# A two-block transformer layer in float32: the norms by token tile, with a token-major slab behind each

## The chip, the cores and the metric

The kernel runs on one NeuronCore of a Trainium2 chip. The metric is the device time of one execution in microseconds. TensorE multiplies matrices, VectorE, ScalarE and GpSimd (POOL) compute beside it, and SyncE (SP) issues the transfers. PSUM has eight banks of 512 float32 columns on 128 partitions.

## The reference

Two transformer blocks run one behind the other over 256 tokens of width 1024, all in float32. The first block has MoBA attention and gated linear attention, and an FFN whose hidden values go through a causal convolution of three taps. A `final_norm_g` norm ends it. The second block begins with a norm of its own, so between the blocks stand two norms in a row. Its mixer has four branches (short convolution, spatial gating, stick-breaking attention, forgetting attention), and its FFN is a SwiGLU.

```python
def rms_norm(x, g):
    xf = x.astype(jnp.float32)
    y = xf * lax.rsqrt(jnp.mean(xf * xf, axis=-1, keepdims=True) + EPS)
    return (y * g.astype(jnp.float32)).astype(x.dtype)

# first block
        x = x + jnp.concatenate([y_moba, y_gla], axis=-1) @ w_out[l]
        hn = rms_norm(x, ffn_norm_g[l])
        h = causal_dwconv(hn @ w_ffn_up[l], conv_w[l], conv_b[l])
        h_gate, h_val = h[..., :D_FF], h[..., D_FF:]
        x = x + (jax.nn.silu(h_gate) * h_val) @ w_ffn_down[l]
    return rms_norm(x, final_norm_g)
# second block
        xn = _rms_norm(h, norm_mix_g[l])
        h = h + _mixer_block(xn, ...)
        h = h + _swiglu(_rms_norm(h, norm_ffn_g[l]), w_ffn_in[l], w_ffn_out[l])
```

## The kernel before

**Slabs.** All large weights arrive as 117 slabs of 1 MB (`STREAM`, 128 x 2048). An "up" slab holds 256 output columns for all 1024 inputs, a "down" slab 256 inputs for all 1024 outputs. Each is split into a high half that the fast float32 product takes exactly (ScalarE, `rnd`, to `hiw`) and the remainder (VectorE, `res`, to `low`). Both are rings of three. A product of two float32 matrices is thus three: high x high, high x low, low x high (`three`). A slab's high half waits until the slab three before it has been used (`consumed`).

**Order.** No planner is at work: each engine's program is written out by hand, in one order per engine, with semaphores between them. What stands later in an engine's program waits for what stands earlier.

**Stages.** In order: in1, out1, norm 1, FFN 1, norm 2, in2 (11 projections sq, sk, sv, fq, ... and 8 early gates), mix2, norm 3, FFN 2, output. FFN slabs are g and v (up, gate and value) and d (down), f = 0 to 10; the order is `FFN_ORDER`. In the FFN an up slab is made feature-major: weights stand, and 512 columns, high and low tokens side by side (`xx`), move (`feature_major_wide`, into two banks, 16 products of 512 columns and 16 of 256). VectorE reduces the two banks. A down slab (`out_slab`) adds to four accumulators, the quarters q = 0 to 3: token tile q // 2 (128 tokens), output half q % 2. A quarter takes 6 products of 512 columns. The last three down slabs, d8, d9, d10, come in a row behind the last up slab. `g_lo_ffn1` says that VectorE has made the low half (`ylo`) of a hidden slab.

**A norm.** `out_slab` gives `first_tile_out` after quarter 1 of its last slab. VectorE adds quarters 0 and 1 to the residual `h`, and quarters 2 and 3 once the whole slab is done. ScalarE squares and sums tile 0 and half of tile 1 (`norm_stats`), VectorE the other half (`norm_tile1`), POOL takes the inverse root (`inverse_roots`), VectorE scales the rows (`norm_scaled`), and TensorE transposes 16 blocks of 128x128 into four banks (`turn`). Ahead of these it multiplies zeros (`keep_clock`; 11, 19 and 13 calls at norms 1, 2 and 3, each two instructions in the trace). Then ScalarE makes the high half with the gain (`norm_turned`, 8 instructions of 128x256) and VectorE the low half. The first slab behind the norm starts as soon as the first pair of blocks is there. Norm 2 is the two norms in one: `weighted` multiplies `h` with `final_norm_g`, both sums of squares are taken, the rows scaled are the weighted ones, and `h` itself is rewritten behind (line 1205). At norm 1 the low split of slab v0 stands ahead of the norm in VectorE's program, at norm 3 between its additions.

Lines that the rows name: 593 ScalarE's high half of the norm; 984 VectorE's low half; 967 the additions to `h`; 939 VectorE's sum of squares; 948 the scaled rows; 1406 the transposes; 1393 the zeros; 932 and 563 the splits of a slab; 1146 the reduce of an up slab; 1182 the low half of y; 1417 to 1419 the three products; 1442 and 1448 the wide ones and their low part; 544 POOL's copies for the forgetting attention, which follow its roots of norm 2; 485 the output.

Of the kernel before, what the change touches and what calls it, by code (L numbers as in the profile page):

```python
# [17 lines left out]
ALU = mybir.AluOpType  # L18
# [5 lines left out]
P = 128  # L24
T = 256
# [31 lines left out]
WARM = [12, 11, 19, 13]  # L57
# [39 lines left out]
def build(nc, x_in, slabs_in, vec_in, cst_in, out):  # L97
    with ExitStack() as ctx:
# [57 lines left out]

        def norm_scale(n, tt):

            return stat(n, 10 + 2 * tt + (n == 2))

# [65 lines left out]

        def take_bank(pe, name):

            b, _, n, _ = lease[name]
            if n:  # L230
                pe.wait_ge(bank_free[b], n)
# [24 lines left out]
        for q in range(4):  # L256
            tenant(f"n1_{q}", (2, 5, 6, 7)[q], 2)
# [13 lines left out]
        for q in range(4):  # L271
            tenant(f"n2_{q}", 4 + q, 2)
        for n, b in (("sq", 0), ("sk", 1), ("sv", 0), ("fq", 6), ("fk", 7), ("fv", 1), ("cc", 0), ("cx", 1), ("cb", 0),
                     ("u", 1), ("v", 0)):
            tenant(n, b, 2 if n in ("fq", "fk") else 1)
# [23 lines left out]
        for q in range(4):  # L299
            tenant(f"n3_{q}", 4 + q, 2)  # L300
# [35 lines left out]
        def consumed(n, i=None):  # L336

            stage, name = STREAM[n]
            if stage in FREE:
# [22 lines left out]
        xs = piece(0, TT, D)  # L362
        hn = piece(12288, TT, D)
# [88 lines left out]
        def _(sp):  # L452
# [37 lines left out]
        def _(pool):  # L490
            me = Chain("pool_step")

            def inverse_roots(n, tt):

                pool.wait_ge(s(f"ssq{tt}_made"), (n + 1) * (1 + tt))
                mean = stat(n, 6 + 2 * tt)
                if tt == 0:
                    me.step(pool, pool.tensor_scalar(mean, stat(n, 0), EPS, None, ALU.add))  # L500
                else:
                    me.step(pool, pool.tensor_tensor(mean, stat(n, 1), stat(n, 2), ALU.add))
                wide = 1
                if n == 2:
                    wide = 2
                    me.step(pool, pool.tensor_scalar(stat(n, 7 + 2 * tt), mean, EPS, None, ALU.mult))
                    me.step(pool, pool.tensor_tensor(stat(n, 7 + 2 * tt), stat(n, 7 + 2 * tt), stat(n, 3 + tt), ALU.add))
                pool.tensor_tensor(stat(n, 10 + 2 * tt, wide), stat(n, 6 + 2 * tt, wide), mhalf[:, 0:wide],
                                   ALU.pow).then_inc(s("rstd_made"), 1)
# [12 lines left out]
            for tt in range(TT):  # L522
                inverse_roots(0, tt)
# [31 lines left out]
        def _(act):  # L555
# [13 lines left out]
            def norm_stats(n):  # L569

                act.wait_ge(*((s("h_made"), 4 * n - 2) if n else (s("x0_in"), 16)))
                def squares(dst, src, k):
                    return act.activation(dst, src, ACT.Square, scale=D ** -0.5, accum_out=stat(n, k))  # L573

                ins = squares(junk, h[:, 0, :], 0)
                if n == 2:
                    me.step(act, ins)
                    act.wait_ge(s("weighted"), 1)
                    ins = squares(junk, xs[:, 0, :], 3)
                ins.then_inc(s("ssq0_made"), 1)  # L580
                act.wait_ge(*((s("h_made"), 4 * n - 1) if n else (s("x1_in"), 16)))
                ins = squares(junk_act, h[:, 1, 0:D // 2], 1)
                if n == 2:
                    act.wait_ge(s("ssq0_made"), n + 1)
                    act.wait_ge(s("weighted"), 2)
                    ins = squares(junk, xs[:, 1, :], 4)
                ins.then_inc(s("ssq1_made"), 1)

            def norm_turned(n):

                for kt in range(KT):
                    act.wait_ge(*full(f"n{n}_{kt // 2}"))
# [11 lines left out]
            norm_stats(0)  # L604
# [5 lines left out]
            norm_turned(0)  # L610
# [129 lines left out]
            norm_stats(1)  # L740
            act.wait_ge(s("vec_rest_in"), 16)
            norm_turned(1)
# [53 lines left out]

            rnd(b2 + 1)
            norm_stats(2)
            norm_turned(2)
# [119 lines left out]
            norm_stats(3)  # L919
            norm_turned(3)  # L920
# [5 lines left out]
        def _(dve):  # L926
# [8 lines left out]
            def norm_tile1(n):  # L935

                dve.wait_ge(*((s("h_made"), 4 * n) if n else (s("x1_in"), 16)))
                half = h[:, 1, D // 2:]
                dve.tensor_tensor_reduce(junk_dve, half, half, 1.0 / D, EPS, ALU.mult, ALU.add,
                                         stat(n, 2)).then_inc(s("ssq1_made"), 1)  # L940

            def norm_scaled(n, tt):

                dve.wait_ge(s("rstd_made"), 2 * n + tt + 1)
                rows = xs if n == 2 else h
# [1008 lines left out]
```

## Time and profile before

| | |
|---|---|
| median of 3 runs | 752.34 us (752.27 to 753.6) |
| profiled execution | 752.77 us |
| its span | 751.0 us |
| TensorE busy (matmul) | 733.1 us, 98% |
| VectorE, ScalarE, POOL busy | 522.2, 374.6, 49.6 us |
| mean granted TensorE clock | 0.998 |
| read from HBM | 126.57 MB, 170 GB/s |

The span runs from the first to the last instruction; 1.8 us of the execution lie outside it. A product's duration in a row contains its pipeline: a 128x512 product is shown as 0.39 us, while the next one starts 0.23 behind it. Steps are therefore read from one start to the next.

### The profile page before, as it was taken

Reading aid. Unit: us, or ns where it says so; the run is one execution under the profiler, and the core shown is the slowest. Engines: PE = TensorE matmul, PEld = TensorE weight load, DVE = VectorE, ACT = ScalarE, POOL = GpSimd, SP = SyncE. Lnnn points to the kernel's source line nnn. Section 1 sums busy time; section 2 is a strip of 40 time slices with the busy share of each in tenths; the row PEclk is TensorE's granted clock in tenths of the full one; section 3 lists DMA queues with packets and bytes.
Section 4 is the critical chain, followed back from the end, with each engine's and each line's share of the span. In section 5 each row is a group of like instructions: output and inputs, shape, how many; then the busy total and the mean of one; then the engine's idle time right before and its main releaser. Section 6 shows DMA issues by size and latency. Waiting matters only on the chain.

```text
span 751.0 us, 11966 instructions
## 1 busy us (share of the span) xinstructions
PE 733.1 (98%) x4786; PEld 658.7 (88%) x4786; DVE 522.2 (70%) x587; ACT 374.6 (50%) x441; POOL 49.6 (7%) x64
## 2 busy tenths in 40 slices
PE   8999999899999999989999999999999999999997
PEld 7999887788888888879989999999978888888886
DVE  6679836689888888886557636675586766656673
ACT  6635466365554545555564554444445434444341
POOL 2456100100000000030000000000010000000000
PEclk9999999999999999999999999999999999999999
DMA  8836334236555555436343444446443655555431
GB/s 341 325 130 198 113 113 169 93 132 225 187 205 175 205 179 190 147 113 217 121 162 127 160 168 168 168 168 224 170 168 113 224 171 202 187 178 213 168 113 56
DMA packets 18810, 129.28 MB, mean 172 GB/s; under 512 B 2256, under 2 KB 2512, under 8 KB 3536
## 3 DMA queue, kind: packets, MB, share of 16 engines
q1 hardware_dynamic: 18768, 128.68, 48.1%
q8 instruction: 32, 0.52, 0.3%
q14 instruction: 10, 0.08, 0.0%
HBM read 126.57 MB, written 1.05 MB: 170 GB/s over the span
## 4 chain that ended last, share of the span: by engine, by line
PE 91%; DVE 5%; ACT 2%; POOL 1%; issue 1%; DMA 1%; POOLq 0%; DVEq 0%; ACTq 0%
PE ps L1442 21%; PE ps L1417 18%; PE ps L1418 18%; PE ps L1419 18%; PE ps L1448 11%; DVE xx L984 1%; DVE low L932 1%; PE ps L1540 1%; DVE h L967 1%; PE ps L1570 1%; DMA h<-in_x 1%; PE ps L1406 0%; ACT arena L573 0%; PE ps L1563 0%; ACT xx L593 0%
## 5 line engine op out<-in xcount | busy, mean ns | idle before, releaser
L932 DVE TENSOR_TENSOR low<-raw,hiw 128x2048 fp32r<-128x2048 f32 x116 | 268.3, 2314 | 117.7 <-ACT hiw L563 116.7
L563 ACT ACTIVATE hiw<-raw 128x2048 fp32r<-128x2048 f32 x116 | 221.9, 1914 | 176.8 <-PE ps L1448 114.9
L1442 PE MATMUL ps<-xx,hiw 128*128 128x512 f32 x704 | 170.8, 394 | 2.8 <-DVE xx L984 2.6
L1442 PEld LDWEIGHTS ps<-xx,hiw 128*128 128x128 f32 x704 | 131.0, 190 | 31.6 <-DVE xx L984 4.3
L1417 PE MATMUL ps<-xx,hiw 128*128 128x256 f32 x512 | 146.7, 286 | 0.5 <-DVE xx L984 0.5
L1418 PE MATMUL ps<-xx,hiw 128*128 128x256 f32 x512 | 144.8, 283 | 0.0
L1419 PE MATMUL ps<-xx,low 128*128 128x256 f32 x512 | 144.8, 283 | 0.0
L1417 PEld LDWEIGHTS ps<-xx,hiw 128*128 128x128 f32 x512 | 97.9, 191 | 2.4 <-issue 1.8
L1418 PEld LDWEIGHTS ps<-xx,hiw 128*128 128x128 f32 x512 | 97.9, 191 | 0.1
L1419 PEld LDWEIGHTS ps<-xx,low 128*128 128x128 f32 x512 | 97.9, 191 | 0.0
L1448 PEld LDWEIGHTS ps<-xx,low 128*128 128x128 f32 x704 | 90.3, 191 | 3.4
L1448 PE MATMUL ps<-xx,low 128*128 128x256 f32 x704 | 91.3, 283 | 0.0
L1417 PE MATMUL ps<-hiw,yhi 128*128 128x512 f32 x208 | 81.6, 392 | 0.5 <-DVE ylo L1096 0.5
L1418 PE MATMUL ps<-low,yhi 128*128 128x512 f32 x208 | 81.2, 390 | 0.0
L1419 PE MATMUL ps<-hiw,ylo 128*128 128x512 f32 x208 | 80.9, 389 | 0.0
L1146 DVE TENSOR_REDUCE arena<-ps 128x512 f32<-128x1024 f32 x44 | 53.8, 1222 | 32.4 <-PE ps L1448 32.3
L601 ACT ACTIVATE arena<-ps 128x512 f32<-128x512 f32 x37 | 22.1, 597 | 99.2 <-PE ps L1419 99.2
L1417 PEld LDWEIGHTS ps<-hiw,yhi 128*128 128x128 f32 x208 | 39.1, 188 | 8.9 <-DVE ylo L1096 0.8
L1419 PEld LDWEIGHTS ps<-hiw,ylo 128*128 128x128 f32 x208 | 39.1, 188 | 8.3
L1418 PEld LDWEIGHTS ps<-low,yhi 128*128 128x128 f32 x208 | 39.1, 188 | 7.3
L1168 DVE SCALAR_TENSOR_TENSOR arena<-arena,vec 128x255 f32<-128x255 f32 x88 | 40.5, 481 | 6.4 <-ACT arena L761 2.2
L1417 PE MATMUL ps<-hiw,xx 128*128 128x256 f32 x112 | 32.3, 288 | 0.0
(199 smaller groups left out, 802.7 us busy)
## 6 DMA issues: line engine op xcount, KB each, us to landing
raw<-in_slabs SPq DMA_DIRECT2D x117, 1024.0 KB, 4.8
vec<-in_vec SPq DMA_DIRECT2D x1, 1258.5 KB, 10.3
cst<-in_cst SPq DMA_DIRECT2D x1, 1220.0 KB, 13.7
h<-in_x SPq DMA_DIRECT2D x2, 512.0 KB, 4.2
arena<-arena SPq DMA_DIRECT2D x16, 64.0 KB, 3.1
out<-h SPq DMA_DIRECT2D x2, 512.0 KB, 2.6
vec<-in_vec SPq DMA_DIRECT2D x1, 229.0 KB, 4.6
cst<-in_cst SPq DMA_DIRECT2D x1, 66.0 KB, 4.3
```

Source lines behind the costliest of these rows:

```text
L563: act.activation(hiw[:, n % SPLIT, :], raw[:, n % RAW, :], ACT.Copy).then_inc(hi_made, 1)
L601: return act.activation(dst, src, func, scale=scale).then_inc(*frees(name))
L932: dve.tensor_tensor(low[:, n % SPLIT, :], raw[:, n % RAW, :], hiw[:, n % SPLIT, :].bitcast(F32), ALU.subtract).then_inc(lo_made, 1)
L967: dve.tensor_tensor(dst, ps[:, acc, :], dst, ALU.add).then_inc(s("h_made"), 1)
L984: dve.scalar_tensor_tensor(out=xlo[:, kt, :], in0=bank(f"n{n}_{kt // 2}")[:, kt % 2 * T:(kt % 2 + 1) * T], scalar=V(f"ng{n}")[:, kt:kt + 1 ...
L1146: dve.tensor_reduce(dst, wide_hidden(j).rearrange("p c (a b) -> p c b a", a=2), AX_X, ALU.add).then_inc(hidden_free(k, f, j)[0], 1)
L1168: ins = dve.scalar_tensor_tensor(out=dst[:, o:], in0=src[:, 0:T - o], scalar=w, in1=dst[:, o:], op0=ALU.mult, op1=ALU.add)
L1417: pe.matmul(o, whi, mhi, start=start, stop=False)
L1418: pe.matmul(o, whi, mlo, start=False, stop=False)
L1419: return pe.matmul(o, wlo, mhi, start=False, stop=stop)
L1442: pe.matmul(banks[:, c, :], hi[:, kt, cc_], xx[:, kt].rearrange("p a b -> p (a b)"), start=kt == 0, stop=False)
L1448: mm = pe.matmul(banks[:, c, 0:T], lo[:, kt, cc_], xhi[:, kt, :], start=False, stop=kt == KT - 1)
```

## The change

Norms 1 to 3 go by token tile. VectorE adds quarter by quarter (`quarter`, on `quarter_out` after quarters 0, 1 and 2), each tile has its own sums, root, rows, transposes and halves, and ScalarE scales half of each tile's rows. Tile 1's eight transposes go to two banks (`turned_at`). The slab behind the norm (`TILED`: g0 of either FFN, sq in in2) is computed token-major, a tile at a time, by 24 products of 256 columns each (`tile_slab`); tile 1's transposes stand between tile 0's high and low products. ScalarE copies the result to SBUF (`rows_out`), and four transposes turn it back (`turn_back`): in the FFNs between v0's high and low products, in in2 between the two tiles of sv. VectorE takes g0 by a copy of 512 columns instead of a reduce. sk's products wait for the high half alone at first (`feature_major_late`). The zeros at norms 1 to 3 are gone.

At norm 2 the squares of `h` are kept (`squared`) and VectorE weights them with the square of `final_norm_g` in its sums; the gain of both norms is one vector, which POOL spreads (`gains`, behind norm 1's roots, with `fg2`) and VectorE joins after its second FFN 1 step. `h` is rewritten by a product of two tensors. FFN 1's d9 and d10 run tile by tile, with tile 0's transposes ahead of d10's last quarter. The output's second tile leaves in two halves.

```diff
-WARM = [12, 11, 19, 13]
+WARM = 12
+TILED = {1: [("ffn1", "g0")], 2: [("in2", "sq")], 3: [("ffn2", "g0")]}
...
             def inverse_roots(n, tt):
+                a = 8 * tt
+                if n == 2:
+                    pool.wait_ge(s("squares_made"), sums_until(n, tt))
...
+                else:
+                    pool.wait_ge(s("squares_made"), sums_until(n, tt))
+                    pool.wait_ge(s("half_summed"), sums_until(n, tt))
+                    me.step(pool, pool.tensor_tensor(stat(n, a + 2), stat(n, a), stat(n, a + 1), ALU.add))
+                    pool.tensor_tensor(norm_scale(n, tt), stat(n, a + 2), mhalf[:, 0:1], ALU.pow)\
+                        .then_inc(s("root_made"), 1)
...
+                if n == 1:
+                    pool.wait_ge(s("vec_rest_in"), 16)
+                    pool.tensor_tensor(gains, V("fg").rearrange("p (k c) -> p k c", k=KT),
+                                       ident.unsqueeze(1).broadcast_to([P, KT, P]), ALU.mult).then_inc(s("gains_spread"), 1)
+                    pool.tensor_tensor(fg2, V("fg"), V("fg"), ALU.mult).then_inc(s("gains_squared"), 1)
...
# ScalarE, norm 1 (norm 3 alike) and norm 2
+            for tt in range(TT):
+                square(1, tt, 0)
+                rows(1, tt)
+                tile_turned(1, tt)
+            for tt in range(TT):
+                rows_out(1, 0, tt)
...
+            for nh in range(2):
+                square(2, 0, nh)
+            rows(2, 0)
+            square(2, 1, 0)
+            tile_turned(2, 0)
+            square(2, 1, 1)
             rnd(b2 + 1)
+            rows(2, 1)
+            tile_turned(2, 1)
...
# VectorE
+            def norm(n, used):
+                quarter(n, 0, used)
+                quarter(n, 1, used)
+                half_sum(n, 0)
+                quarter(n, 2, used)
+                rows(n, 0)
+                quarter(n, 3, used)
+                half_sum(n, 1)
+                tile_turned(n, 0, range(0, 4))
+                rows(n, 1)
+                tile_turned(n, 0, range(4, 8))
+                tile_turned(n, 1, range(8))
+            def weighted_norm(used):
+                quarter(2, 0, used)
+                quarter(2, 1, used)
                 for nh in range(2):
+                    weighted_sum(0, nh)
+                quarter(2, 2, used)
+                rows(2, 0)
+                tile_turned(2, 0, range(0, 4))
+                quarter(2, 3, used)
+                tile_turned(2, 0, range(4, 8))
+                for nh in range(2):
+                    weighted_sum(1, nh)
+                rows(2, 1)
+                tile_turned(2, 1, range(8))
...
+            norm(1, (proj_used["out1"], 4))
             res(first_ffn + 1)
-            norm(1, (proj_used["out1"], 4))
             res(first_ffn + 2)
...
# TensorE
+            def tile_slab(norm, i, tt, middle=None):
+                name, n = f"rows{norm}_{i}_{tt}", AT[TILED[norm][i]]
+                hi, lo = slab_views(n, KT)
+                t_ = slice(tt * P, (tt + 1) * P)
+                take_bank(pe, name)
+                o = bank(name)[:, 0:256]
+                pe.wait_ge(lo_made, n + 1)
+                for kt in range(KT):
+                    if kt % 2 == 0:
+                        pe.wait_ge(s("xhi_made"), KT + 16 * (norm - 1) + 8 * tt + kt + 2)
+                    pe.matmul(o, xhi[:, kt, t_], hi[:, kt, :], start=kt == 0, stop=False)
+                    pe.matmul(o, xhi[:, kt, t_], lo[:, kt, :], start=False, stop=False)
+                if middle is not None:
+                    middle()
+                for kt in range(KT):
...
+                    mm = pe.matmul(o, xlo[:, kt, t_], hi[:, kt, :], start=False, stop=kt == KT - 1)
+                mm.then_inc(*fills(name))
...
+            def ffn_up_first(k):
+                norm, n = {"ffn1": 1, "ffn2": 3}[k], AT[(k, "v0")]
+                turn_tile(norm, 0)
+                tile_slab(norm, 0, 0, lambda: turn_tile(norm, 1))
+                tile_slab(norm, 0, 1)
+                def back():
+                    pe.wait_ge(*hidden_free(k, 0, 0, done=False))
+                    turn_back(norm, 0, wide_hidden(0)[:, 0, :]).then_inc(hidden_full(k, 0, 0)[0], 1)
...
+                feature_major_wide(wide_hidden(1), n, (lo_made, n + 1), back).then_inc(hidden_full(k, 0, 1)[0], 1)
...
+            def ffn_down_last_two(k):
+                for tt in range(TT):
+                    for f in (FF - 2, FF - 1):
+                        n, par = AT[(k, f"d{f}")], f % 2
+                        pe.wait_ge(s(f"g_lo_{k}"), f + 1)
+                        pe.wait_ge(lo_made, n + 1)
+                        for q in (2 * tt, 2 * tt + 1):
+                            if q == 3 and f == FF - 1:
+                                turn_tile(2, 0)
+                            mm = out_quarter(n, q, (2 * par, 2 * par + 1), yhi, ylo, bank(f"{k}_acc{q}"), False,
+                                             f == FF - 1)
```

## Rows read from the trace of the kernel before

**Rows 1.** The page, part 1: busy time, share and instructions of each engine.
```profile
PE 733.1 (98%) x4786; PEld 658.7 (88%) x4786; DVE 522.2 (70%) x587; ACT 374.6 (50%) x441; POOL 49.6 (7%) x64
```

**Rows 2.** The page, part 4: the chain that ended last, by engine.
```profile
PE 91%; DVE 5%; ACT 2%; POOL 1%; issue 1%; DMA 1%; POOLq 0%; DVEq 0%; ACTq 0%
```

**Rows 3.** Timeline, norm 3: start us, us, engine line op tiles xcount [idle before].
```profile
553.50 1.29 DVE L967 TENSOR_TENSOR h<-ps,h 128x512 f32<-128x512 f32 x2 [0.92 <-PE ps L1419]
...
555.82 0.39 PE L1419 MATMUL ps<-hiw,sml 128*128 128x512 f32 x1
...
558.84 0.08 DVE L939 DVE_READ_ACCUMULATOR2_ANT st<- 128x1 f32 x1
...
560.17 0.88 DVE L948 TENSOR_SCALAR arena<-h,st 128x512 f32<-128x512 f32 x2 [0.45 <-POOL st L508]
...
560.71 1.09 PE L1406 MATMUL ps<-cst,arena 128*128 128x128 f32 x8 [0.17 <-DVE arena L948]
...
561.18 3.02 ACT L593 ACTIVATE xx<-ps,vec 128x256 fp32r<-128x256 f32 x8 [2.84 <-PE ps L1406]
...
562.05 3.22 DVE L984 SCALAR_TENSOR_TENSOR xx<-ps,vec,xx 128x256 fp32r<-128x256 f32 x8 [1.01 <-ACT xx L593]
...
567.73 2.08 PE L1448 MATMUL ps<-xx,low 128*128 128x256 f32 x16
...
569.65 3.82 PE L1442 MATMUL ps<-xx,hiw 128*128 128x512 f32 x16
```

**Rows 4.** Timeline, norm 1, TensorE.
```profile
134.62 2.62 PE L1393 MATMUL ps<-zeros 128*128 128x128 f32 x22
...
141.51 6.29 PE L1442 MATMUL ps<-xx,hiw 128*128 128x512 f32 x16 [1.33 <-DVE xx L984]
...
149.55 0.63 PE L1442 MATMUL ps<-xx,hiw 128*128 128x512 f32 x2
```

**Rows 5.** Windows, TensorE, after norms 1 and 3: PE busy (instructions), granted clock, DMA.
```profile
144.00:146.00 2.00, 2.00 (x5) 0.50 0.00 0
564.00:566.00 2.00, 1.90 (x7) 1.00 0.04 8
```

**Rows 6.** Timeline, the end of FFN 1 and norm 2.
```profile
320.87 0.19 PEld L1417 LDWEIGHTS ps<-hiw,yhi 128*128 128x128 f32 x1 [0.26 <-DVE ylo L1182]
...
326.20 0.39 PE L1419 MATMUL ps<-hiw,ylo 128*128 128x512 f32 x1
...
332.34 2.21 POOL L544 COPY arena<-cst 128x1024 f32<-128x1024 f32 x2
...
332.42 2.41 DVE L948 TENSOR_SCALAR arena<-arena,st 128x512 f32<-128x512 f32 x2 [0.88 <-POOL st L508]
...
342.03 0.28 PE L1417 MATMUL ps<-xx,hiw 128*128 128x256 f32 x1
```

**Rows 7.** Groups by line and shape: count, busy us, mean ns, idle before.
```profile
L601 ACT ACTIVATE arena<-ps 128x512 f32<-128x512 f32 x37 | 22.1, 597 | 99.2 <-PE ps L1419 99.2
...
L534 POOL TENSOR_TENSOR arena<-arena 128x256 f32<-128x256 f32 x8 | 5.5, 682 | 36.8 <-ACT arena L601 20.1 <-PE ps L1540 15.9 <-PE ps L1537 0.9
```

**Rows 8.** Timeline, the start of FFN 1.
```profile
155.79 1.22 DVE L1146 TENSOR_REDUCE arena<-ps 128x512 f32<-128x1024 f32 x1
...
164.13 0.68 DVE L1182 TENSOR_TENSOR ylo<-arena,yhi 128x512 fp32r<-128x512 f32 x1
...
166.25 0.40 PE L1417 MATMUL ps<-hiw,yhi 128*128 128x512 f32 x1
...
178.06 0.68 DVE L1182 TENSOR_TENSOR ylo<-arena,yhi 128x512 fp32r<-128x512 f32 x1
```

**Rows 9.** Timeline, fq's first product.
```profile
354.50 0.39 PE L1417 MATMUL ps<-xx,hiw 128*128 128x256 f32 x1
```

**Rows 10.** Timeline, the last additions.
```profile
746.61 1.29 DVE L967 TENSOR_TENSOR h<-ps,h 128x512 f32<-128x512 f32 x2 [1.43 <-PE ps L1419]
```

**Rows 11.** The line of the output DMA, landing time.
```profile
DMA to landing us min/median/max: 2.6/2.6/2.6
```

More of the change, by code:

```diff
@@ L298, in build @@
             tenant(f"w2_{q}", q, 0)
-        for q in range(4):
-            tenant(f"n3_{q}", 4 + q, 2)
+        for q in range(6):
+            tenant(f"n3_{q}", (4, 5, 6, 7, 2, 3)[q], 2 if q < 4 else 4)
+        for tt in range(TT):
+            tenant(f"rows3_0_{tt}", tt)
         ffn_tenants("ffn2")
@@ L338, in consumed @@
             stage, name = STREAM[n]
+            for norm, slabs in TILED.items():
+                if (stage, name) in slabs:
+                    return full(f"rows{norm}_{slabs.index((stage, name))}_1")
             if stage in FREE:
@@ L918, in _ @@
             rnd_to(AT[("ffn2", "g0")] + 1)
-            norm_stats(3)
-            norm_turned(3)
+            for tt in range(TT):
+                square(3, tt, 0)
+                rows(3, tt)
+                tile_turned(3, tt)
+            for tt in range(TT):
+                rows_out(3, 0, tt)
             rnd_to(AT[("ffn2", "g0")] + 2)
@@ L1190, in ffn @@
                 ffn_step(k, 1)
+                if k == "ffn1":
+                    dve.wait_ge(s("gains_spread"), 1)
+                    me.step(dve, dve.tensor_reduce(gain, gains, AX_X, ALU.add))
+                    dve.tensor_tensor(V("ng2"), V("ng2"), gain, ALU.mult).then_inc(s("gains_joined"), 1)
                 with dve.Fori(0, FFN_PAIRS) as i:
@@ L1379, in _ @@
                     res_to(AT[("mix2", f"o{m - 1}")] + (3 if m < 3 else 2))
[L1380 to L1381 removed]
+            norm(3, (proj_used["mix2"], 4))
             res_to(AT[("ffn2", "g0")] + 2)
             ffn("ffn2")
[L1384 removed]
+            for q in range(4):
+                quarter(4, q, (down_used["ffn2"], FF))
         @block.tensor
@@ L1410, in turned, with turn_back @@
+            def turn_back(norm, i, o):
+                for tt in range(TT):
+                    pe.wait_ge(*given_back(f"rows{norm}_{i}_{tt}"))
+                for tt in range(TT):
+                    for c in range(2):
+                        mm = pe.transpose(o[:, c * T + tt * P:c * T + (tt + 1) * P],
+                                          rows_of[norm][i][:, tt, c * P:(c + 1) * P], ident)
+                return mm
             def turned(n, kt):
@@ L1444, in feature_major_wide @@
                 pe.wait_ge(*low_made)
+                if middle is not None:
+                    middle()
                 for c in range(2):
```

345 lines of the change are left out of this document (215 added, 130 removed).

## The prediction

> **What bounds the kernel now.** I read the engines' busy shares first: TensorE is busy for 733.1 of 751.0 us [rows 1]. The chain of work that ended last then says whether it is also the path: 91% of it is TensorE, 5% VectorE [rows 2]. So time is to be had only where TensorE idles or repeats zeros: the three norms between stages. There I read the timeline. At norm 3 the last product starts at 555.82 and, at 0.23 a step, is issued by 556.05; v0 starts at 569.65 [rows 3]. Of these 13.60 us, g0 needs only 16 x 0.227 + 1.92 = 5.55. At norm 1 the same stretch runs from 134.62 to 149.55, 14.93 us [rows 4]: 1.3 more, as the clock fell to its lower level (granted 0.50, which is 1.2 GHz) [rows 5] after 4.3 us in which TensorE had only 16 transposes (the zeros end at 137.24, g0's first product starts at 141.51) [rows 4]. At norm 2 the last product is issued by 326.43, and sq's slab ends with sk's first product at 342.03 [rows 6].
>
> The time is the sum against the profiled execution, 752.77 us (span 751.0 and 1.8 around it), 0.43 above the median of 752.34; I carry it to the median.
>
> **Prices.** 128x256 product: (569.65 - 567.73)/16 = 0.12 [rows 3]. 128x512 product: (326.20 - 320.87 - 0.1)/23 = 0.227, 0.1 being the late start's own delay [rows 6]. Transpose: (1.09 - 0.27)/7 = 0.117 [rows 3]. ScalarE from PSUM takes 0.60 at 512 columns [rows 7] and 3.02/8 = 0.38 at 256 [rows 3], so I take 0.27 for the new 128x128 pieces; VectorE's, 3.22/8 = 0.40 at 256 [rows 3], also 0.27. The bounds are 0.19 (half of the wide one) and 0.38 (no cheaper than it). From the end of VectorE's sum to the scaled rows' start, through two POOL instructions, it is 558.92 to 560.17 = 1.25; rows to first transpose 0.54, first transpose to ScalarE 0.47, 0.22 more where four must be made first [rows 3].
>
> **Norm 3.** With t from 556.05: VectorE can add h's second half at 553.50 as before [rows 3] and its first ahead of that, the half sum ends at 554.95, the root comes at t+0.15. Rows, then 8 transposes from t+0.7. ScalarE turns tile 0 in 8 x 0.27, t+1.15 to t+3.3, and only then squares tile 1 (0.60 as the 512-column copy and 0.1 for reading the sum, t+4.05). POOL: t+5.3. Transposes t+5.85 to t+6.75; ScalarE t+6.55 to t+8.7; VectorE's last four wait for its eighth piece and end at t+9.95; TensorE's last products t+10.35. Against 13.60 that is 3.25 earlier. Turning back costs 4 x 0.117, 0.45. The zeros go, at no gain of their own, since they lay inside waits. v0's low split moves behind the norm: 2.3 on VectorE under v0's 3.65 of high products, free. FFN 2's first down slab keeps about 2.5 us of cover. **Gain 2.8**; with pieces at 0.19 it is 4.0, at 0.38 it is 1.2.
>
> **Norm 1.** The same schedule puts v0 at 134.62 + 10.35 = 144.97, 4.1 better net than 149.55. Most is given back. Before, v0's low split ran ahead of the norm, and VectorE was ready for v0's reduce as it filled (155.79); it finished d0's low y at 164.81, 9.0 later, and TensorE took d0 at 166.25, so there were 1.4 us of slack [rows 8]. Now VectorE leaves the norm at 144.6, does v0's split (2.29), waits for g1's rounding (ScalarE free at 145.5, done 147.4), splits g1, copies g0 (0.65), splits v1 (2.29) and does four conv taps (1.9): reduce of v0 at 154.5, d0 at 163.5. TensorE would stand before d0 at 162.0. That is a gain of 2.7 before POOL is counted. POOL now starts two 128x1024 products right when it has written tile 1's root, which is when VectorE scales tile 1's rows. The row: beside POOL's copies two such scalings took 2.41 [rows 6] instead of 0.88 [rows 3], 0.76 more each. At that price the gain is 1.9. If VectorE waits for all of a POOL product of 1024 columns, 4 x 0.68 = 2.7 [rows 7], of which some 0.1 passes before VectorE comes, 0.1 is left. Bounds 0.1 and 2.7; nothing excludes the waiting, the copies being the shorter instruction, so I take **0.6**.
>
> The Trainium skill bears on this: SBUF — State Buffer, in the part on the shared port pair, says that a VectorE instruction in a two-port mode and a GpSimd instruction exclude each other for the whole instruction. The copies' row agrees: each scaling lasts about one copy (1.14) plus little. By that rule norm 1 would give 0.1; by the row's addition, 1.9.
>
> The gains' join (a reduce over 1024 columns, about 1.2, and a small product) lies on VectorE after its second FFN step: the low y there is begun at 178.06 and TensorE wants it 16.6 (two wide slabs, one down slab) behind 166.25 [rows 8], 4 us of cover. Free; uncovered it would be 1.3.
>
> **Norm 2**, the place where I expect a loss. d9 and d10 now run tile by tile, so d10's first quarter is due after d9's second, at 320.88 - 12 x 0.227 = 318.15 (before, d9 was over at 320.88). But d10's y is split late: in the trace VectorE's low y is what releases TensorE at 320.87 [rows 6]. Now TensorE idles 2.7 us. Onward: d10 q0, q1 end at 323.6, d9 q2, q3 at 326.4, d10 q2 at 327.8. VectorE, in its own order, adds q2 and only then scales tile 0: transposes 329.2, q3 done 331.5. Then q3's add, four low pieces, ScalarE's last square (332.4 to 333.1) and, in line behind it, sk's rounding (to 335.0), two weighted sums (335.0), POOL (336.3), the rows beside POOL's copies as now (0.44 + 0.76), transposes at 337.5. ScalarE's pieces to 340.4, VectorE's to 341.7, sq done 342.1: no earlier than the 342.03 of before. sk shares bank 1 with tile 1's rows, so it waits for ScalarE to empty them (0.38 and two hand-overs): sk at 342.8, 0.7 late. VectorE then has sk's split, two 128x1024 products for h (1.2 each instead of 0.7) and sv's split: sv 0.25 late, and its middle carries the 0.45 of turning back. sq is therefore full at 352.1 instead of 342. ScalarE empties sq before it rounds fq (0.5, then 1.9, then VectorE's 2.3): fq's low half is ready at 357.1. TensorE has left sv at 354.9 and stick-breaking's scores at 356.3, so fq starts at 357.2 instead of 354.50 [rows 9]. **Loss 2.7**, and nothing behind it gives time back, as TensorE is the chain from there on. If ScalarE and VectorE caught up it would be 1.1 (bank 0.7, turning back 0.45); with pieces at 0.38, 4.5.
>
> **End.** The last adds start at 746.61 and take 0.64 each; the output waited for both and landed 2.6 after its issue [rows 10, 11]. Now one add (0.65 earlier) and half the bytes follow the last product: gain 0.65 if landing is all latency, 1.3 if half of it is bytes. I take **1.0**.
>
> **Clock.** No zeros are issued at norms 1 to 3 any more. At norm 2 TensorE idles from 333.4 to 337.5, then has 8 transposes: 5 us without a product. In the trace 4.3 us with only transposes brought the lower level at norm 1, while norm 3, built alike, kept 1.00 [rows 5]. A fall costs 14.93 - 13.60, 1.3 to 1.5, where TensorE is the bound [rows 3, 4]; at norm 1 it now falls into the wait before d0. I take **0.7 lost**, about half a fall.
>
> The Trainium skill, TensorE: Matmul & The Clock Gate, part on PE-mode transpose, holds that transposes do not count as busy for the gate. By it norm 2's stretch is as bare as norm 1's was and the fall comes: 0.8 more.
>
> **Sum:** -0.6 - 2.8 + 2.7 - 1.0 + 0.7 = -1.0: 751.8 in the profiled execution, **751.3** as median.
>
> **Rivals.**
> 1. *Norm 2's debt is hidden.* The loss stays at 1.1, POOL costs 0.76 only, the clock holds. For: an in2 slab gives ScalarE 2.5 and VectorE 2.3 of work in TensorE's 5.8; against: their order is fixed, and sq comes before fq. -1.9 - 2.8 + 1.1 - 1.0 = -4.6; with the debt whole and the rest so, -3.0. Between them 748.9.
> 2. *Slower: the clock falls at both norms 2 and 3.* Place: the first slab after each; price 1.5 twice; it decides once both fall while norm 1 yields under 1. -0.1 - 2.8 + 2.7 - 0.65 + 3.0 = +2.2: 754.5 (the wait before d0 hides a fall at norm 1); with pieces above 0.3, more. For: 7 us at norm 3 with only 16 paced products and no zeros; against: there it held through the transposes of before [rows 5].
> 3. *POOL blocks VectorE for whole products* (the rule above): norm 1 yields 0.1, else as forecast: 751.8.
>
> **Chances.** Forecast 0.42 (own range 749.9 to 752.8), rival 1 0.28, rival 2 0.18, rival 3 0.12. What a measurement of this kernel tells from no change is 0.2%, 1.5 us: below 750.8 lie rival 1 and a third of the forecast, 0.43; above 753.8 most of rival 2, 0.17; between them 0.40. Range 748.3 to 754.3.
>
> **What would show it.** Right: an idle of 2.7 before d10's first quarter with the low y as releaser; v0 about 10.4 after the last product at norm 3; a wait before d0 in FFN 1; fq's start released by its own low split. Wrong: no wait before fq (rival 1), granted clock 0.50 after norm 3 (rival 2), tile 1's scaling at norm 1 longer than 2 us (rival 3), or ScalarE's 128x128 pieces far from 0.27.

## The result, and the profile after

The changed kernel takes 753.74 us (median of 17, 752.22 to 755.14); the kernel before, on the same chip, 752.24 (17, 750.90 to 753.60). The ratio is 1.0019, 95% interval 1.0010 to 1.0028: slower by 1.5 us, where 1.0 us faster was forecast. The profiled execution took 753.39 us, span 751.4. Part 1 of its page, then part 4, the chain by engine:

```profile
PE 725.6 (97%) x4744; PEld 653.8 (87%) x4744; DVE 525.0 (70%) x615; ACT 382.4 (51%) x477; POOL 52.3 (7%) x70
```

```profile
PE 87%; DVE 6%; ACT 3%; issue 1%; POOL 1%; DMA 1%; POOLq 0%; DVEq 0%; ACTq 0%
```

TensorE is busy 7.5 us less than before [rows 1] and the span did not shrink: zeros have become waits, and its share of the chain fell from 91 to 87% [rows 2]. The waits of TensorE name them (us in total, times, longest):

```profile
PE ps L1546 <- DVE arena L1067: 10.5, 6, 4.0
PE ps L1589 <- DVE ylo L1306: 3.8, 2, 2.6
```

L1546 is the turn of a tile, L1067 VectorE's half of its scaled rows, L1306 FFN 1's low y. The longest of each stand side by side at norm 2. TensorE's timeline there (start, us, ... [idle before <- releaser]):

```profile
316.77 0.39 PE L1591 MATMUL ps<-hiw,ylo 128*128 128x512 f32 x1
319.71 0.50 PE L1589 MATMUL ps<-hiw,yhi 128*128 128x512 f32 x1 [2.55 <-DVE ylo L1306]
...
322.60 0.63 PE L1589 MATMUL ps<-hiw,yhi 128*128 128x512 f32 x1
...
329.73 1.06 PE L1546 MATMUL ps<-cst,arena 128*128 128x128 f32 x8 [1.27 <-DVE arena L1067]
...
338.13 1.92 PE L1546 MATMUL ps<-cst,arena 128*128 128x128 f32 x8 [4.04 <-DVE arena L1067]
339.70 2.03 PE L1569 MATMUL ps<-hiw,xx 128*128 128x256 f32 x8
...
345.07 3.14 PE L1630 MATMUL ps<-xx,hiw 128*128 128x256 f32 x24 [0.47 <-ACT arena L657]
...
359.32 0.35 PE L1589 MATMUL ps<-xx,hiw 128*128 128x256 f32 x1 [0.92 <-DVE low L1012]
```

d10 idles 2.55 before its first quarter; fq starts 4.8 later than before [rows 9]. And equal instructions have two durations: 8 transposes take 1.06 at 329.73 and 1.92 at 338.13, the 128x512 products 0.39 and 0.63. The windows say why. In each line the third number from the end is the granted clock as a share of 2.4 GHz; 0.50 is the lower level, 1.2 GHz:

```profile
320.00:322.00 2.00, 2.00 (x8) 1.56 (x8) 2.00 (x2) 0.00 (x0) 0.00 (x0) 0.77 0.83 287
322.00:324.00 2.00, 2.00 (x6) 1.51 (x6) 0.46 (x1) 0.72 (x2) 0.00 (x0) 0.50 0.97 307
...
338.00:340.00 2.00, 1.87 (x9) 1.90 (x10) 0.00 (x0) 0.76 (x3) 0.89 (x1) 0.54 0.00 0
340.00:342.00 2.00, 2.00 (x13) 2.00 (x12) 1.59 (x7) 1.65 (x7) 0.00 (x0) 0.61 0.00 0
```

A stretch at the lower level is called a fall here. There are two, both at norm 2, each of 3 to 4 us. The kernel before has one in its trace, at norm 1 [rows 5], and none at norm 2.

Norm 3 went as forecast. The last product ahead of it is issued by 560.83:

```profile
566.15 1.06 PE L1546 MATMUL ps<-cst,arena 128*128 128x128 f32 x8 [1.39 <-DVE arena L1067]
...
570.88 3.83 PE L1613 MATMUL ps<-xx,hiw 128*128 128x512 f32 x16
574.54 0.60 PE L1578 MATMUL ps<-cst,arena 128*128 128x128 f32 x4
```

v0 comes after 10.05 us instead of 13.60 [rows 3], and the turn back costs 0.36. At norm 1 the timeline of all engines shows VectorE's half rows of tile 0, then of tile 1 beside GpSimd's two products of the gains:

```profile
134.59 0.49 DVE L1067 TENSOR_SCALAR arena<-h,st 128x512 f32<-128x512 f32 x1 [0.38 <-POOL st L550]
...
139.33 2.00 POOL L587 TENSOR_TENSOR arena<-vec,cst 128x1024 f32<-128x1024 f32 x1
...
139.40 2.21 DVE L1067 TENSOR_SCALAR arena<-h,st 128x512 f32<-128x512 f32 x1 [1.94 <-POOL st L550]
...
141.28 2.08 POOL L589 TENSOR_TENSOR arena<-vec 128x1024 f32<-128x1024 f32 x1
```

0.49 against 2.21 for the same instruction. v0 starts at 146.49 (149.55 before [rows 4]) and d0 at 165.02 (166.25 [rows 8]).

From milestone to milestone of the two traces: norm 1 gives 1.2, norm 2 costs 6.0 (fq 359.32 - 354.50, plus the 1.2 that it inherits), norm 3 gives 3.1, the end 1.25: together the 0.4 by which the spans differ. In what follows each execution's mean granted clock is told with its time, since it takes discrete values and the time goes with it. Of the kernel before, 60 executions beside the experiments: 751.09 us at 1.00 (5 executions), 752.3 at 0.997 to 0.998 (29), 753.5 at 0.995 (19). The profiled ones with their clocks fit it: each fall takes 0.002 to 0.003 off the mean. Of the changed kernel's 17 executions 8 are at 0.995 (753.14 us), 6 at 0.993 (754.37) and 3 at 0.991 (755.09). The profiled one, with its two falls, is thus one of the 8; the median execution has lost more clock, and no trace shows where.

Two traces can also differ by up to 0.7 us before anything that the change touches: the first transposes of the kernel, at 7 to 8 us, start at 7.90 in the changed kernel's profile and at 7.16 in that of experiment 5. Differences between traces are therefore taken over a stretch.

### The profile page after: what moved, and what is told of

Same layout as the page of the kernel before. It is cut to its first block, busy times and chain, and to the rows that moved or that the text cites. A ratio compares the mean times of both kernels' runs of the same rounds, so it can differ in the third digit from the quotient of the medians.

```text
span 751.4 us, 11991 instructions
## 1 busy us (share of the span) xinstructions
PE 725.6 (97%) x4744; PEld 653.8 (87%) x4744; DVE 525.0 (70%) x615; ACT 382.4 (51%) x477; POOL 52.3 (7%) x70
## 4 chain that ended last, share of the span: by engine, by line
PE 87%; DVE 6%; ACT 3%; issue 1%; POOL 1%; DMA 1%; POOLq 0%; DVEq 0%; ACTq 0%
PE ps L1613 18%; PE ps L1589 17%; PE ps L1590 17%; PE ps L1591 17%; PE ps L1621 10%; DVE low L1012 2%; ACT hiw L610 1%; PE ps L1569 1%; PE ps L1735 1%; PE ps L1546 1%; DVE arena L1067 1%; ACT xx L650 1%; PE ps L1765 1%; PE ps L1630 1%; DMA h<-in_x 1%
## 5 line engine op out<-in xcount | busy, mean ns | idle before, releaser
L1613 PE MATMUL ps<-xx,hiw 128*128 128x512 f32 x672 | 159.9, 390 | 0.0
L1613 PEld LDWEIGHTS ps<-xx,hiw 128*128 128x128 f32 x672 | 124.5, 188 | 24.8
L1589 PE MATMUL ps<-xx,hiw 128*128 128x256 f32 x480 | 137.3, 286 | 0.9 <-DVE low L1012 0.9
L1590 PE MATMUL ps<-xx,hiw 128*128 128x256 f32 x480 | 135.8, 283 | 0.0
L1591 PE MATMUL ps<-xx,low 128*128 128x256 f32 x480 | 135.8, 283 | 0.0
L1589 PEld LDWEIGHTS ps<-xx,hiw 128*128 128x128 f32 x480 | 91.8, 191 | 2.5 <-issue 2.1
L1590 PEld LDWEIGHTS ps<-xx,hiw 128*128 128x128 f32 x480 | 91.8, 191 | 0.1
L1591 PEld LDWEIGHTS ps<-xx,low 128*128 128x128 f32 x480 | 91.8, 191 | 0.0
L1621 PEld LDWEIGHTS ps<-xx,low 128*128 128x128 f32 x672 | 86.0, 191 | 3.1
L1621 PE MATMUL ps<-xx,low 128*128 128x256 f32 x672 | 87.3, 283 | 0.0
L1270 DVE TENSOR_REDUCE arena<-ps 128x512 f32<-128x1024 f32 x42 | 51.3, 1221 | 24.7 <-PE ps L1621 24.6
L828 ACT ACTIVATE arena<-arena,vec 128x256 f32<-128x256 f32 x44 | 23.9, 591 | 23.5 <-DVE arena L1270 21.9
```

The source lines that it names most:

```text
L828: act.activation(yb[par][:, 2 * j + c, :], hid[par][j][:, c, :], ACT.Identity, scale=sc, bias=bi).then_inc(s("tap2"), 1)
L1270: ins = dve.tensor_reduce(dst, wide_hidden(j).rearrange("p c (a b) -> p c b a", a=2), AX_X, ALU.add)
L1589: pe.matmul(o, whi, mhi, start=start, stop=False)
L1590: pe.matmul(o, whi, mlo, start=False, stop=False)
L1591: return pe.matmul(o, wlo, mhi, start=False, stop=stop)
L1613: pe.matmul(banks[:, c, :], hi[:, kt, cc_], xx[:, kt].rearrange("p a b -> p (a b)"), start=kt == 0, stop=False)
```

## The experiments

Each ran in five rounds beside the kernel before, whose median was 753.29 us for the first four, 752.31 for the next four and 752.49 for the last. Its executions at clock 1.00 took 750.86, 751.12 and 751.09 us in the three sets (medians of 3, 1 and 1), so times at equal mean clock can be compared between the sets, medians less well.

**1. Zero products back in norm 2's waits.**
```
+ if tt == 0 and f == FF - 1: keep_clock("n2_0", 10)    # ahead of d10's wait
- tile_slab(2, 0, 0, lambda: turn_tile(2, 1))
+ tile_slab(2, 0, 0, turn_warm)                         # keep_clock("n2_4", 17); turn_tile(2, 1)
```


> The changed kernel with products of the zero tile put back in front of two of norm 2's waits: 10 of them ahead of the wait for d10's low part (idle 2.55 us at 317.17) and 17 ahead of turn_tile(2, 1) (idle 4.04 us at 334). Theory: after both waits the granted clock fell (321.0 to 324.3 and 338.1 to 341.4), and the products run at half rate there cost some 1.6 and 1.8 us; with TensorE kept busy in the waits the clock stays at 1.00 and the time falls by 3.3 us against the changed kernel, to about 750.4. Rival: the slowed products are hidden by the chain behind them (VectorE's quarter adds, rows and quantised low parts, then the slab's hi by ScalarE), and the time stays within 0.5 us, 753.2 to 754.2.

Measured 751.67 us, 0.9983 (0.9971 to 0.9995): by the medians 2.1 below the changed kernel; each against its own kernel before, 1.0019 and 0.9983, it is 2.7. The zeros sit inside the waits:

```profile
318.48 2.39 PE L1521 MATMUL ps<-zeros 128*128 128x128 f32 x20
321.19 0.50 PE L1589 MATMUL ps<-hiw,yhi 128*128 128x512 f32 x1 [0.32 <-DVE ylo L1306]
...
333.77 3.96 PE L1521 MATMUL ps<-zeros 128*128 128x128 f32 x34
...
337.96 1.06 PE L1546 MATMUL ps<-cst,arena 128*128 128x128 f32 x8 [0.24 <-DVE arena L1067]
```

The clock is 1.00 from 316 to 344. But this execution has a fall at norm 1 that the changed kernel's profile lacks, behind the same wait of 3.12 us:

```profile
142.00:144.00 2.00, 2.00 (x13) 2.00 (x12) 1.04 (x5) 1.66 (x7) 1.28 (x1) 0.57 0.00 0
144.00:146.00 2.00, 2.00 (x12) 2.00 (x12) 2.00 (x8) 0.90 (x4) 0.00 (x0) 0.57 0.00 0
```

The one execution without any fall took 749.64. That is 3.5 below the changed kernel at 0.995, for two falls. The clock theory holds; the 3.3 was too much for the median, since another fall is still free to come.

**2. The last two down slabs whole again.**
```
- for tt in range(TT):
-     for f in (FF - 2, FF - 1):
-         for q in (2 * tt, 2 * tt + 1):
+ for f in (FF - 2, FF - 1):
+     for q in range(4):
```


> The changed kernel with the last two down slabs of FFN 1 slab by slab again (q0 to q3 of d9, then of d10), the turn of tile 0 still ahead of d10's q3; the rest as changed. Theory: d10's g_lo then comes while d9's 24 products run, so the wait of 2.55 us at 317.17 and the fall of the clock behind it (1.6 us) go, while tile 0's rows come some 5 us later against the end of d10 and the wait at turn_tile(2, 0) grows from 1.27 us to about 3 to 4. Net against the changed kernel: between -2.5 and +1 us, about 752.7, with the clock at 1.00 from 317 to 328. Rival: tile by tile hides as much of norm 2 as it costs, and whole slabs are slower by 2 us or more (755.7 and above).

Measured 753.75 us, 1.0011 (0.9999 to 1.0023): by the medians no difference from the changed kernel. The wait at d10 is gone and the clock is 1.00 to 328, as the first theory has it; but the turn of tile 0 waits 3.35 us, and the clock then falls between 330 and 344. The wait moved and took its fall along. This execution has a fall at norm 1 too (granted 0.61 and 0.54 from 142 to 146). At equal mean clock experiment 2 is 0.4 to 1.0 below the changed kernel (752.71 against 753.14 at 0.995, 753.39 against 754.37 at 0.993); more of its executions are at the low clocks.

**3. GpSimd's products of the gains after norm 1.**
```
+ pool.wait_ge(s("g_lo_ffn1"), 1)
  pool.tensor_tensor(gains, V("fg")..., ident..., ALU.mult)
```


> The changed kernel, with GpSimd's two 128x1024 products of the gains (2.00 and 2.08 us at 139.33 and 141.28) kept until FFN 1's first low part is made (about 168 us), past norm 1. Theory (port): VectorE's scaling of tile 1's half row took 2.21 us beside them against 0.49 for the same instruction of tile 0; with them gone it takes 0.49, TensorE's turn of tile 1 starts 1.7 us earlier, and the time falls by 1.0 to 1.7 us, to about 752.3. Rival: TensorE's slab behind norm 1 is then held by the next low part or by something else, and less than 0.4 us comes back although the half row takes 0.49.

Measured 751.33 us, 0.9984 (0.9972 to 0.9997); at a mean clock of 0.995 it is 751.27 against 753.14 for the changed kernel, 1.9 less. Timeline, both half rows and the products in their new place:

```profile
138.88 0.49 DVE L1068 TENSOR_SCALAR arena<-h,st 128x512 f32<-128x512 f32 x1 [1.93 <-POOL st L550]
...
162.79 0.47 PE L1590 MATMUL ps<-hiw,yhi 128*128 128x512 f32 x1 [1.24 <-DVE ylo L1307]
...
163.59 3.23 DVE L1013 TENSOR_TENSOR low<-raw,hiw 128x2048 fp32r<-128x2048 f32 x1
...
164.63 3.94 POOL L590 TENSOR_TENSOR arena<-vec 128x1024 f32<-128x1024 f32 x1
```

d0 starts at 162.79 instead of 165.02. Of these 2.23 us 0.50 lie ahead of norm 1 (its first transposes start at 134.72 instead of 135.22), so the collision cost 1.73, which is 2.21 - 0.49. It is not gone: VectorE's split takes 3.23 instead of 2.29, its four conv taps behind that 3.54 instead of 1.91, and GpSimd's product 3.94 instead of 2.08, where TensorE does not wait for them.

**4. Norm 2 as before, norms 1 and 3 and the output as changed.**
```
- TILED = {1: [("ffn1", "g0")], 2: [("in2", "sq")], 3: [("ffn2", "g0")]}
+ TILED = {1: [("ffn1", "g0")], 3: [("ffn2", "g0")]}
... # pre-weighted rows, 19 zero products, feature-major sq, whole d9 and d10; no products of the gains
```


> The changed kernel with everything of norm 2 as before (norm over both tiles with the pre-weighted rows, feature-major sq, whole d9 and d10, 19 zero products, no products of the gains on GpSimd); norms 1 and 3 and the output in three parts as changed. Theory (from the milestones of the two traces): norm 1 gave 1.2 us, norm 3 3.15, the end 1.25, norm 2 cost 6.0; without norm 2's part the time is 752.24 - 5.6 = 746.6, and without the products of the gains beside norm 1 up to 1.7 less, 745. Rival: the gains at norms 1 and 3 are given back later by the low parts of the following slabs, and the time is 750 or more.

Measured **745.93 us**, 0.9914 (0.9894 to 0.9933): faster than before by some 6.5 us, and with experiment 7 the best kernel of the study. At clock 1.00 it is 745.25 (three of six executions), the kernel before 751.09: norms 1 and 3 and the end are worth 5.8, and nothing of it is given back.

**5. Experiments 1 and 3 together.**

> Both edits at once: the zero products in norm 2's two waits, and GpSimd's products of the gains kept until after norm 1. Theory (two separate costs): the half row beside GpSimd (1.9 us, runs at the same clock) and the falls of the clock (about 1.7 us each, two at norm 2, and with GpSimd late no wait of 3 us is left at norm 1 to bring one there). They add: 747.8 in runs with the clock at 1.00 throughout, median 747.8 to 749.5. What then stays against the kernel with the old norm 2 (745.25 at clock 1.00) is the price of the tiled norm 2 itself: about 2.5 us. Rival: the tiled norm 2 costs nothing by itself once the clock holds, and this kernel comes within 1 us of 745.9.

Measured 748.35 us, 0.9944 (0.9926 to 0.9962); 748.18 at clock 1.00, where five of six executions were. The two costs add within 0.5 us: 753.14 less 3.5 for two falls and less 1.9 is 747.7. At equal clock 2.9 us are left to experiment 4: the tiled norm 2 by itself, with sq token-major and d9 and d10 tile by tile. The two timelines show them, first this kernel:

```profile
314.51 2.39 PE L1522 MATMUL ps<-zeros 128*128 128x128 f32 x20
317.23 0.50 PE L1590 MATMUL ps<-hiw,yhi 128*128 128x512 f32 x1 [0.32 <-DVE ylo L1307]
...
325.59 1.06 PE L1547 MATMUL ps<-cst,arena 128*128 128x128 f32 x8 [1.27 <-DVE arena L1068]
...
333.98 1.07 PE L1547 MATMUL ps<-cst,arena 128*128 128x128 f32 x8 [0.23 <-DVE arena L1068]
...
339.36 4.10 PE L1631 MATMUL ps<-xx,hiw 128*128 128x256 f32 x32 [0.47 <-ACT arena L658]
351.75 0.70 PE L1927 MATMUL ps<-arena 64*128 64x256 f32 x4 [0.19 <-ACT arena L665]
353.59 0.36 PE L1590 MATMUL ps<-xx,hiw 128*128 128x256 f32 x1 [0.92 <-DVE low L1013]
```

and experiment 4's:

```profile
323.14 4.40 PE L1567 MATMUL ps<-zeros 128*128 128x128 f32 x38
327.92 1.09 PE L1968 MATMUL ps<-cst,arena 128*128 128x128 f32 x8 [0.38 <-DVE arena L1369]
...
332.80 0.35 PE L1635 MATMUL ps<-xx,hiw 128*128 128x256 f32 x1 [0.54 <-DVE xx L1373]
```

With the old norm 2, sk could start 9.66 + 48 x 0.12 = 15.4 us after d10's last product. In the tiled one 36 products of 0.227 were left at 314.51, so the same point is 322.7, and sk starts 16.7 behind it: 1.3 late. Turning back takes 0.36 and the two last waits 1.1, in sum 2.7.

The same rows price the falls in the traces, as the work between them is the same in the changed kernel. From d10's first product to the turn of tile 0 it is 8.36 us here and 10.02 there (319.71 to 329.73); from the turn of tile 1 to sk 5.38 here and 6.94 there (338.13 to 345.07). The two falls cost 1.7 and 1.6.

**6. The same with whole down slabs,** 13 zero products ahead of each turn of norm 2.

> As the kernel with both edits, but the last two down slabs whole again, and 13 zero products ahead of each turn of norm 2 (waits of 3.35 and 3.42 us without them). Theory: without d10's early wait (2.55 us) and with the longer one at the turn of tile 0 (3.35 against 1.27 us) the idle time is the same within 1 us, so with the clock held the order of the slabs is worth little: within 1 us of the kernel with both edits, on the fast side by up to 1. Rival: tile by tile hides tile 0's norm, and whole slabs cost 2 us more (750 and above).

Measured 748.67 us, 0.9942 (0.9924 to 0.9961), 747.75 at clock 1.00. With the clock held too, the order of the two slabs is worth little: 0.4 in favour of whole slabs, from two executions against five. What tile by tile hides of tile 0's norm it seems to lose to d10's low y.

**7. Experiment 4 with zero products ahead of the turns of tile 1.**

> The kernel with the old norm 2 and the new norms 1 and 3, with 5 zero products ahead of the turn of tile 1 at norms 1 and 3 (waits of 1.39 and 1.40 us) and 5 ahead of tile 1's turn at norm 2 (wait of 1.42 us). Theory: the runs of that kernel at a mean clock of 0.995 to 0.998 (746.6 to 747.7, against 745.25 at 1.00) have falls behind one of these waits; filled, more runs come at 1.00, and the median falls from 745.9 towards 745.2. Rival: the falls are elsewhere, and the zero products do nothing or delay their turns by up to 0.4 us each: 745.9 to 747.

Measured 745.93 us, 0.9907 (0.9888 to 0.9927), as without them: half of the executions at 1.00, half at 0.998. The rival is right. The profiled one has its fall at 6 to 12 us, before any norm.

**8. GpSimd's copies after norm 2 as well.**
```
+ pool.wait_ge(s("xhi_made"), KT + 32)
  for j, dst in enumerate((fqp, fkp)): pool.tensor_copy(dst, ...)
```


> As the kernel with both edits, with GpSimd's two copies of 2.2 us each, which began at 336.67 beside the scaling of tile 1's half row at norm 2, kept until ScalarE has turned all of that norm. Theory (port): that half row took 1.23 us beside them against 0.48 for tile 0's; it takes 0.49 again and the turn of tile 1 starts 0.75 us earlier: 0.5 to 0.8 us less than the kernel with both edits. Rival: ScalarE's half row (0.72 us) and the turn's other needs end as late, and nothing comes back.

Measured 748.40 us, 0.9949 (0.9932 to 0.9966), no difference from experiment 5 (748.03 and 748.18 at clock 1.00). The two copies take 2.21 us together, not 2.2 each. The port theory is right on the row and wrong on the time:

```profile
332.78 0.49 DVE L1069 TENSOR_SCALAR arena<-h,st 128x512 f32<-128x512 f32 x1 [1.46 <-POOL st L545]
...
333.77 1.04 PE L1548 MATMUL ps<-cst,arena 128*128 128x128 f32 x8
...
336.64 4.20 POOL L593 COPY arena<-cst 128x1024 f32<-128x1024 f32 x2 [3.89 <-ACT xx L652]
...
339.85 2.06 DVE L1334 SCALAR_TENSOR_TENSOR h<-h,st,vec 128x1024 f32<-128x1024 f32 x1
```

The row takes 0.49 instead of 1.23, but the copies now meet VectorE's products for h (2.06 for the first, 1.2 each elsewhere), ahead of sv's split: TensorE got a new wait of 0.35 for it. The experiment has a flaw as well: the 17 zero products, 3.96 us of them, fitted the wait of 4.04 and now outlast the shorter one. The turn has no wait in front of it any more and comes 3.80 us after the first zero instead of 4.18. So of the 0.75 only 0.4 could reach TensorE, and the wait of 0.35 took that back; what the whole 0.75 would give, no run shows.

**9. Experiment 4 with norm 3 as before too.**

> The kernel with the old norm 2 and the new norms 1 and 3 (745.9 median, 745.25 at clock 1.00), with norm 3 and the first slab of FFN 2 as before too. Theory (milestones): norm 3 tile by tile gave 3.1 us, from mix2's last product to FFN 2's v0; without it 748.4 at clock 1.00, median 748.4 to 749.5. Rival: much of it was given back later by the low parts of FFN 2, and the time rises by less than 1.5 us.

Measured 749.82 us, 0.9965 (0.9952 to 0.9979); 748.44 at clock 1.00, 3.2 above experiment 4. The theory's 3.1 holds.

**10. Experiment 4 with the output in two DMAs.**

> The kernel with the old norm 2 and the new norms 1 and 3, its output sent in two DMAs of a tile (the last of 512 KB) instead of three. Theory: the last DMA is issued at the same time and lands after 2.7 us instead of 2.0, and the last add's start does not change: 0.6 to 0.7 us more, and, if the quarter-wise adds give the rest of the end's 1.25 us, no more than that: 745.9 + 0.65 = 746.5. Rival: the whole 1.25 us is the DMA's, and it is 747.2.

Measured 747.70 us, 0.9936 (0.9921 to 0.9950); no execution had the clock at exactly 1.00, so the medians, 1.8 apart, don't give the term. The traces do: from the last product's start (740.28) to the span's end (744.5) it is 4.22; with three DMAs it is 3.58 (739.82 to 743.4), 0.64 less. The last DMA of 256 KB lands after 2.0 us, the one of 512 KB after 2.6 to 2.7. The other 0.46 between the two traces lies ahead of the last product. The rest of the end's 1.25 fits the one add that no longer follows the last product (0.65).

**11. Experiment 3 with zero products ahead of d10 only.**

> The changed kernel with GpSimd's products after norm 1, and the zero products only ahead of d10's wait, none ahead of the turn of tile 1. Theory (each wait brings its own fall): the clock holds from 316 to 333 and falls once behind the wait of some 4 us at the turn, worth about 1.7 us: 749.9, between the kernel without zero products (751.3) and the one with both (748.3). Rival: one fall hangs on the other, and either both go (748.3) or the second grows to take the first one's place (751).

Measured 750.45 us, 0.9970 (0.9958 to 0.9981); 749.72 at 0.997 (two executions), 1.5 above experiment 5 at 1.00. The other five are at 0.995 (750.49), with more clock lost than the profiled one shows. The timeline and the windows of the unfilled wait:

```profile
326.36 1.06 PE L1547 MATMUL ps<-cst,arena 128*128 128x128 f32 x8 [1.27 <-DVE arena L1068]
334.76 1.94 PE L1547 MATMUL ps<-cst,arena 128*128 128x128 f32 x8 [4.03 <-DVE arena L1068]
```

```profile
334.00:336.00 2.00, 1.24 (x6) 1.27 (x7) 0.61 (x1) 0.21 (x2) 1.52 (x2) 0.61 0.00 0
336.00:338.00 2.00, 2.00 (x12) 2.00 (x11) 0.94 (x4) 2.00 (x8) 0.00 (x0) 0.53 0.03 8
```

The fall behind the unfilled wait is there and the one at d10 is not: of these two, each wait brings its own fall. From the turn of tile 1 to sk it is 6.81 here (334.76 to 341.57) against 5.38 in experiment 5, 1.4 more.

**12. Experiment 5 with ScalarE rounding two slabs before it empties sq and sk.**
```
- elif IN2[k] in ("sq", "sk", ...): evacuate(...)
- rnd(b2 + k + 3)
+ rnd(b2 + k + 3)
+ if k == 1: evacuate("sq", sqT); evacuate("sk", skT)
```


> The changed kernel with both edits (zero products, GpSimd's products late), and ScalarE rounds the next two slabs before it takes sq and sk from PSUM. There it was idle for 6.31 us before sq's turn back was full, and TensorE then waited 0.92 us for the low part of fq's slab (0.19 us more at the stick scores). Theory: the late turn of sq costs this wait through ScalarE's order; with the slabs rounded first the waits go, and the time falls by 0.8 to 1.1 us, from 748.35 to 747.4. Rival: the stick scores now wait for sk's copy, behind sq's, and nothing or a loss up to 0.6 us comes out.

Measured 748.11 us, 0.9940 (0.9925 to 0.9956); 747.15 at clock 1.00 (two executions) against 748.18, 1.0 less, and neither of the two waits is in the trace. On the median it shows as 0.2 only, as fewer executions kept the clock.

## Why the prediction was wrong

**The step that failed is the clock term, "0.7 lost, about half a fall".** The trace has two whole falls at norm 2 in its place. They cost 1.7 and 1.6 us there, 3.2 together (experiment 5's rows against the changed kernel's); experiment 1, where zeros fill both waits, took 749.64 us in its one execution without a fall, against 753.14 with two. The prediction weighed only the wait from 333 to 337 and put a half on it. It had worked out the 2.7 us of the wait at d10 itself, and did not ask whether TensorE would come out of that at the same clock. Filling that wait alone kept the clock from 316 to 334 (experiment 11). The median execution lost more clock than these two falls; where, no trace shows.

**The rest of the sum was right within 1 us, and on the cautious side.** Without its clock term it gives 1.7 less than a kernel before that has one fall, 750.6 as median. The changed kernel without falls is at 750.0 by the balance below, and at 749.64 in the one execution of experiment 1.

**The base carried a fall of its own.** The sum ran against an execution at 0.998 with the fall at norm 1. Of norm 1's 1.2 in the traces about that much is this fall: without it the kernel before takes 751.09 instead of 752.3. Against a base at held clock the changed norm 1, with GpSimd's products beside it, gains nothing: by the balance it loses 0.5.

At held clock the balance is, in us: norm 3 -3.2 (experiment 9), end -1.25 (traces; 0.64 of it experiment 10), norm 1 without GpSimd -1.4 (what is left of 5.8), GpSimd's products +1.9 (experiment 3; 1.7 in its trace), norm 2's tiling +2.9 (experiment 5 against 4). That is -1.0, 750.0, and two falls of 1.5 to 1.7 make 753.0 to 753.4; the changed kernel at its best clock of 0.995 measured 753.14. Norm 1's -1.4 is a remainder, not measured by itself.

The other steps:
- *Norm 3, gain 2.8*: 3.1 to 3.2. v0 after 10.05 for 10.35 forecast. Right, and so the 0.27 for a 128x128 piece: eight take 2.18 on ScalarE (row at 135.67 of the trace) and 2.16 on VectorE.
- *Norm 1, 0.6*: 1.2 in the traces. Without GpSimd d0 was forecast at 163.5; in experiment 3 it came at 162.79, which is 163.3 when the 0.50 ahead of norm 1 are added back. GpSimd's price at d0 is 1.7, between the 0.8 and the 2.6 that I had set: the wait is for one whole product, and that took 2.00, not the 2.7 taken from four of 256 columns. Rival 3's mechanism is real: the half row ended 0.28 us after GpSimd's first product, at 141.61 and 141.33.
- *Norm 2, loss 2.7*: 2.9 at held clock, with its parts: 2.55 idle for 2.7, sk 1.3 late, fq released by its own low split with a wait of 0.92 (357.2 - 356.3 in the forecast). That ScalarE's order is the cause of this wait is shown by experiment 12. That the order of d9 and d10 is not what costs is shown by 2 and 6.
- *End, 1.0*: 1.25.
- *Rival 2, slower by the clock* had the mechanism and about the size (754.5 for two falls, 753.7 measured), but the place wrong: norm 3 kept 1.00, both falls are at norm 2. That its total came near is in part luck, as it had norm 1 at 0.1 and the end at 0.65 and the median execution lost more than two falls. Rival 1 fell: norm 2's debt came in full.

The Trainium skill's page SBUF — State Buffer, part on the shared port pair, says that VectorE in a two-port mode and GpSimd exclude each other for the whole instruction. The trace agrees with it, 2.21 beside a product of 2.00, and the row of the two copies, from which I had priced 0.76, agreed as well: those are 1.1 each. By that rule norm 1's price was to be read from GpSimd's instruction's length, not from another collision.

The same skill's TensorE: Matmul & The Clock Gate says in its part on PE-mode transpose that transposes do not count as busy in the same way. The two falls at norm 2 do not test that: the one at 338.13 was there when the first transpose began, after 4.04 us without any instruction. The prediction went by norm 1, where 4.3 us with only transposes were followed by a fall. It passed over the same stretch at norm 2 of the kernel before, which is longer and was not:

```profile
326.43 4.40 PE L1393 MATMUL ps<-zeros 128*128 128x128 f32 x38
331.30 1.06 PE L1406 MATMUL ps<-cst,arena 128*128 128x128 f32 x8 [0.47 <-DVE arena L948]
333.71 0.66 PE L1406 MATMUL ps<-cst,arena 128*128 128x128 f32 x4 [1.35 <-DVE arena L948]
334.89 0.66 PE L1406 MATMUL ps<-cst,arena 128*128 128x128 f32 x4 [0.52 <-DVE arena L948]
336.08 0.36 PE L1417 MATMUL ps<-xx,hiw 128*128 128x256 f32 x1 [0.54 <-DVE xx L984]
```

```profile
332.00:334.00 2.00, 0.65 (x7) 0.41 (x6) 1.58 (x2) 0.00 (x0) 2.00 (x3) 1.00 0.00 0
334.00:336.00 2.00, 1.03 (x8) 0.55 (x6) 1.77 (x4) 1.81 (x6) 0.56 (x1) 1.00 0.00 0
336.00:338.00 2.00, 1.92 (x15) 1.93 (x16) 2.00 (x6) 2.00 (x5) 0.00 (x0) 1.00 0.03 8
```

From 330.83 to 336.08, 5.25 us, TensorE had 16 transposes and nothing else, and the clock stayed at 1.00. So such a stretch brings a fall in one place and not in another; what decides it, no run here shows.

## What to carry over

Where an edit opens a wait on TensorE or takes zero products out of one, price the wait and the clock behind it separately: here a wait of 2.55 or 4.04 us cost 1.4 to 1.7 more after it was over, and zeros laid inside it cost nothing as long as they were shorter than the wait (experiment 8 has them longer). Before taking a sum against one profiled execution, look at the windows for a fall that the base already has. Splitting a stage into tiles paid at norm 3 (3.2 us) and cost 2.9 at norm 2. My reading is the length of the chain per tile: two GpSimd instructions at norm 3, two weighted sums and six GpSimd steps at norm 2, where the turn of tile 1 waited 4 us. No experiment changed that length by itself.

## What the hardware showed that I had not expected

- *The same sequence falls in one execution and not in the next.* After the wait of 3.12 us at norm 1 the changed kernel's profile kept 1.00, experiment 1's fell to 0.57 and experiment 2's to 0.54. Some executions fall where there is no norm (6 to 12 us, 80 to 86 us). So a kernel's times lie in steps, 1.2 us for the kernel before, and its median moves with how many executions hold the clock: 751.09, 752.3 and 753.5 for the kernel before.
- *A collision of VectorE and GpSimd can slow either, and moving it moves the collision.* GpSimd's product went from 2.08 to 3.94 and VectorE's split from 2.29 to 3.23 (experiment 3); two copies from 2.21 to 4.20 (experiment 8).
